# One transformer block pair on one core: the last 64 tokens' expert rows gathered by index and summed by VectorE

## What is computed

```
q = (h @ w_q)                              # per token and head, two halves of 128
s = q . subkeys                            # 16 score rows of 128 per token
v, i = top_k(s, 16)                        # per score row
cand = v[0][:, None] + v[1][None, :]       # 256 pairs per head
tv, tj = top_k(cand, 16)
eidx = i[0] * 128 + i[1] at tj             # 128 experts per token
w = softmax(tv)
a = gelu(h . w_down[eidx])
out = sum over the picks of (w * a) * w_up[eidx]
x = x + gate * out ; result = rms_norm(x) * g
```

## Time and profile before

| | us |
|---|---|
| runs of the kernel, median of 3 | 1251.74 |
| lowest and highest run | 1247.74, 1253.19 |
| span of the profiled execution | 1246.6 |
| TensorE busy | 1197.3 |
| VectorE busy | 900.8 |
| ScalarE busy | 619.8 |
| GpSimd busy | 548.6 |
| down stage with selection, 474 to 886 us | 412.0 |
| up stage, 886 to 1232 us | 346.0 |

### The profile page before, as it was taken

The page is one execution under the profiler, slowest core; times in us unless marked ns, Lnnn a source line. Parts: engine busy times, 40 slices in busy tenths (PEclk is TensorE's granted clock), DMA queues, the critical chain, the costliest instruction groups (busy, mean ns, idle before and its releaser), DMA issues.

```text
span 1246.6 us, 19173 instructions
## 1 busy us (share of the span) xinstructions
PE 1197.3 (96%) x7224; PEld 1047.8 (84%) x7224; DVE 900.8 (72%) x1844; ACT 619.8 (50%) x1079; POOL 548.6 (44%) x323
## 2 busy tenths in 40 slices
PE   4999999999998999999999999999999999999996
PEld 2778877776776899999999999999888888888885
DVE  5678656787886626999668999999566656656666
ACT  1545444454635435444556665555545545545453
POOL 0887759584533015888867777766200000000000
PEclk9999999999999999999999999999999999999998
DMA  9978764354421542555545555444566667666654
GB/s 377 416 315 341 283 275 172 136 210 148 186 89 68 216 155 88 186 185 186 182 142 166 155 158 165 153 153 153 169 227 228 191 224 227 192 190 192 195 193 152
DMA packets 54523, 244.28 MB, mean 196 GB/s; under 512 B 6944, under 2 KB 7328, under 8 KB 42016
## 3 DMA queue, kind: packets, MB, share of 16 engines
q1 hardware_dynamic: 54000, 242.34, 56.3%
q10 hardware_dynamic: 432, 0.72, 0.2%
HBM read 240.94 MB, written 2.10 MB: 195 GB/s over the span
## 4 chain that ended last, share of the span: by engine, by line
PE 88%; DVE 6%; issue 2%; POOL 1%; ACT 1%; DMA 1%; SPq 0%; POOLq 0%; DVEq 0%; ACTq 0%
PE bank L1546 10%; PE bank L1547 10%; PE bank L1550 10%; PE banks L1586 5%; PE bank L1586 5%; PE bank L1589 5%; PE banks L1592 5%; PE bank L1592 5%; PE banks L1589 5%; PE banks L1560 3%; PE banks L1140 2%; PE banks L1146 2%; PE bank L1140 2%; PE bank L1146 2%; PE banks L1152 2%; PE bank L1152 2%
## 5 line engine op out<-in xcount | busy, mean ns | idle before, releaser
L769 POOL TENSOR_TENSOR split_r<-ring,split_r 128x1024 fp32r<-128x1024 f32 x128 | 307.6, 2404 | 156.6 <-ACT split_r L823 156.6
L823 ACT ACTIVATE split_r<-ring 128x1024 fp32r<-128x1024 f32 x256 | 269.1, 1052 | 182.4 <-PE bank L1550 182.4
L1546 PE MATMUL bank<-h_high_r,split_r 128*128 128x256 f32 x1024 | 252.3, 284 | 0.7 <-issue 0.7
L1547 PE MATMUL bank<-h_low_r,split_r 128*128 128x256 f32 x1024 | 252.0, 284 | 0.0
L2170 DVE TENSOR_TENSOR split_r<-ring,split_r 128x1024 fp32r<-128x1024 f32 x128 | 156.8, 1225 | 65.6 <-ACT split_r L823 65.6
L1546 PEld LDWEIGHTS bank<-h_high_r,split_r 128*128 128x128 f32 x1024 | 197.3, 193 | 0.9 <-ACT G L993 0.9
L1547 PEld LDWEIGHTS bank<-h_low_r,split_r 128*128 128x128 f32 x1024 | 197.6, 193 | 0.0
L773 POOL TENSOR_TENSOR small<-small 128x1 f32<-128x1 f32 x2 | 1.5, 760 | 358.7 <-DVE small L2196 358.7
L744 POOL TENSOR_TENSOR wq_low_r<-G,G_r 128x512 fp32r<-128x512 f32 (+1 forms) x104 | 135.0, 1333 | 47.8 <-ACT G_r L818 47.8
L1550 PE MATMUL bank<-h_high_r,split_r 128*128 128x256 f32 x1024 | 143.7, 283 | 0.0
L1059 ACT ACTIVATE gs_r<-G 128x256 fp32r<-128x256 f32 x128 | 53.5, 418 | 172.6 <-PE bank L1592 172.6
(11 more groups left out here) (444 smaller groups left out, 2234.1 us busy)
## 6 DMA issues: line engine op xcount, KB each, us to landing
ring<-in_down SPq DMA_DIRECT2D x128, 512.0 KB, 3.5
ring<-in_up SPq DMA_DIRECT2D x128, 512.0 KB, 3.5
G<-in_ada SPq DMA_DIRECT2D x32, 1024.0 KB, 10.3
G<-in_in SPq DMA_DIRECT2D x32, 1024.0 KB, 7.0
G<-in_out SPq DMA_DIRECT2D x8, 1024.0 KB, 7.1
G<-in_wq SPq DMA_DIRECT2D x8, 1024.0 KB, 7.6
tab<-in_ada SPq DMA_DIRECT2D x4, 1024.0 KB, 6.3
G<-in_poolup SPq DMA_DIRECT2D x2, 1024.0 KB, 6.0
```

Source lines behind the costliest of these rows:

```text
L769: pool.tensor_tensor(wsplit[:, j % SPLIT, 1, :], raw[:, j % RAW, :], wsplit[:, j % SPLIT, 0, :].bitcast(F32), ALU.subtract).then_inc(low_r ...
L823: nc.scalar.activation(wsplit[:, n % SPLIT, 0, :], raw[:, n % RAW, :], ACT.Copy).then_inc(high_ready, 1)
L1546: mm(o, w[0][:, c, :], h_high[:, c, :], start=(c == 0), stop=False)
L1547: mm(o, w[0][:, c, :], h_low[:, c, :], start=False, stop=False)
```

## The change

The last 64 of 256 tokens (`FEW`) leave the dense up stage; 192 (`TD`) stay.

- The one-hot weights are built for 192 tokens only: 48 batches instead of 64, from column 44 (`J0`) instead of 53. So the selection is wanted nine columns earlier.
- `top16` takes two searches at a time and interleaves their steps, so that each step waits for the last but one instruction instead of the last.
- In the down stage ScalarE writes the activations of the last 64 tokens to a small buffer of 8 columns (`stage`), which SyncE stores to HBM (`z_few`, 256 KB each, 16 stores).
- VectorE names the picks of these tokens: row numbers of `w_up` and places in `z_few` (`name_few`; 128 partitions = 2 groups of 64 picks x 64 tokens).
- GpSimd issues 64 transfers by index of 128 rows of 4 KB (`fetch_row`, 512 KB each, 6 buffers; six of them in the down stage) and 64 of 128 single numbers (`take`).
- VectorE multiplies and adds each fetched row to `row_sum` (`add_row`, 128x1024), in 64 of the columns 8 to 118, folds the two groups at columns 122 and 124.
- The up stage has 10 matmuls per column: the first 128 tokens keep three products for each column half; for the other tokens one 128-wide operand holds the high parts of 64 tokens and their low parts side by side, and two products per half give all. The low part of the activations is written by two instructions, 64 and 128 wide.
- Of the 128 low parts of the weights GpSimd writes each third, VectorE the others.
- At the end the second token half comes first, with a copy by ScalarE and an addition by VectorE for each of its column halves.

```diff
@@ -47,13 +47,28 @@
 RAW = 4
 SPLIT = 2
 BATCH = 4
-NB = T // BATCH
-J0 = 53
+FEW = 64
+TD = T - FEW
+REP = P // FEW
+NB = TD // BATCH
+J0 = 44
+STAGE = 8
+ROW_BUFFERS = 6
+TAKE = 8
+SUM_COLUMN = [8 + 7 * k // 4 for k in range(FEW)]
+EARLY_ROW = [100 + 2 * k for k in range(ROW_BUFFERS)]
+ROW_COLUMN = [SUM_COLUMN[k] + 1 for k in range(FEW - ROW_BUFFERS)]
+TAKE_COLUMN = [1 + k // 2 for k in range(TAKE)]
+TAKE_COLUMN += [SUM_COLUMN[TAKE * (k // TAKE - 1)] + 1 + k % TAKE for k in range(TAKE, FEW)]
+FOLD_COLUMN = 122
+LATE_ORDER = [(1, 0), (1, 1), (0, 0), (0, 1)]
 LAST_BATCH = P - 4
 GATE_LOAD = [10 + 16 * k for k in range(4)]
 GATE_SUM = [20 + 16 * k for k in range(4)]
 GATE_ROW = [48, 80]
 GATE_ADD = [54, 86]
+POOL_UP = [n for n in range(P) if n % 3 == 2]
+DVE_UP = [n for n in range(P) if n % 3 != 2]
...
                 if n - RAW < P:
                     sp.wait_ge(low_ready, n - RAW + 1)
                 else:
-                    sp.wait_ge(up_low, n - RAW - P + 1)
+                    wait_up_low(sp, n - RAW - P)
                 src = d["down"][n] if n < P else d["up"][n - P]
                 sp.dma_start(raw[:, n % RAW, :], src).then_inc(raw_in[n % RAW], 16)
+                if RAW + STAGE - 1 <= n < P + RAW and (n - RAW + 1) % STAGE == 0:
+                    m = (n - RAW + 1) // STAGE - 1
+                    sp.wait_ge(gelu_done, STAGE * (m + 1))
+                    sp.dma_start(z_few[:, m * STAGE:(m + 1) * STAGE, :], stage[:, m % 2]).then_inc(z_stored[m % 2], 16)
...
+            def fetch_row(k):
+
+                b = k % ROW_BUFFERS
+                if k == 0:
+                    pool.wait_ge(few_named, 3 * REP)
+                    pool.wait_ge(selT_full, 1)
+                if k >= ROW_BUFFERS:
+                    pool.wait_ge(row_used, k - ROW_BUFFERS + 1)
+                pool.indirect_dma_start(row_buffer[b], None, up_rows,
+                                        bass.IndirectOffsetOnAxis(ap=row_id.bitcast(U32)[:, k:k + 1], axis=0)).then_inc(row_fetched[b], 16)
+
+            def take(k):
+
+                m = k // TAKE
+                if k == 0:
+                    for half in range(2):
+                        pool.wait_ge(z_stored[half], 16 * (P // STAGE // 2))
+                if k % TAKE == 0 and m >= 2:
+                    pool.wait_ge(few_weighed, m - 1)
+                pool.indirect_dma_start(row_z[:, k:k + 1], None, z_cells,
+                                        bass.IndirectOffsetOnAxis(ap=z_id.bitcast(U32)[:, k:k + 1], axis=0)).then_inc(z_taken[m % 2], 16)
...
-            for t in range(NT):
-                pool.wait_ge(var_ready, 6 + t)
+                if j in EARLY_ROW:
+                    fetch_row(EARLY_ROW.index(j))
+            for n in range(P):
+                if n in POOL_UP:
+                    pool.wait_ge(high_ready, P + n + 1)
+                    pool.tensor_tensor(wsplit[:, n % SPLIT, 1, :], raw[:, n % RAW, :], wsplit[:, n % SPLIT, 0, :].bitcast(F32),
+                                       ALU.subtract).then_inc(up_low_pool, 1)
+                for k in range(FEW):
+                    if TAKE_COLUMN[k] == n:
+                        take(k)
+                if n in ROW_COLUMN:
+                    fetch_row(ROW_BUFFERS + ROW_COLUMN.index(n))
+            for k, t in enumerate((1, 0)):
+                pool.wait_ge(var_ready, 6 + k)
...
+                    nc.scalar.activation(zbuf[:, 0:done], src[:, 0:done], ACT.Gelu_apprx_tanh)
+                if done < TD:
+                    nc.scalar.activation(Gv[:, j, done:TD], src[:, done:TD], ACT.Gelu_apprx_tanh)
+                if j % STAGE == 0 and m >= 2:
+                    act.wait_ge(z_stored[m % 2], 16 * (m // 2))
+                ins = nc.scalar.activation(stage[:, m % 2, j % STAGE, :], src[:, TD:T], ACT.Gelu_apprx_tanh)
...
+            def up_parts(n):
+
+                g, w = gs[n % 2], wsplit[:, n % SPLIT]
+                first, both, first_low = g[:, 0:P], g[:, P:2 * P], g[:, 2 * P:3 * P]
+                halves = [(half, slice(half * 512, (half + 1) * 512)) for half in range(2)]
+                return first, both, first_low, w, halves
+
             def up(n):
 
-                outs = [(ps[4 + 2 * t + half][:, :], slice(t * P, (t + 1) * P), slice(half * 512, (half + 1) * 512))
-                        for t in range(NT) for half in range(2)]
-                g, w = gs[n % 2], wsplit[:, n % SPLIT]
+                first, both, first_low, w, halves = up_parts(n)
                 pe_.wait_ge(gs_high, n + 1)
                 pe_.wait_ge(high_ready, P + n + 1)
-                for k, (o, tok, cols) in enumerate(outs):
-                    if n == 0 and k == 2:
-                        pe_.wait_ge(z_done, late_columns(P - 1))
-                    mm(o, g[0][:, tok], w[:, 0, cols], start=(n == 0), stop=False, skip_group_check=True)
-                pe_.wait_ge(gs_low, n + 1)
-                for o, tok, cols in outs:
-                    mm(o, g[1][:, tok], w[:, 0, cols], start=False, stop=False, skip_group_check=True)
-                pe_.wait_ge(up_low, n + 1)
-                for o, tok, cols in outs:
-                    ins = mm(o, g[0][:, tok], w[:, 1, cols], start=False, stop=False, skip_group_check=True)
+                for half, cols in halves:
+                    mm(ps[4 + half][:, :], first, w[:, 0, cols], start=(n == 0), stop=False, skip_group_check=True)
+                if n == 0:
+                    pe_.wait_ge(z_done, late_columns(P - 1))
+                pe_.wait_ge(gs_low, 2 * n + 1)
+                for half, cols in halves:
+                    mm(ps[6 + half][:, :], both, w[:, 0, cols], start=(n == 0), stop=False, skip_group_check=True)
+                pe_.wait_ge(gs_low, 2 * n + 2)
+                for half, cols in halves:
+                    mm(ps[4 + half][:, :], first_low, w[:, 0, cols], start=False, stop=False, skip_group_check=True)
+                wait_up_low(pe_, n)
+                for half, cols in halves:
+                    mm(ps[4 + half][:, :], first, w[:, 1, cols], start=False, stop=False, skip_group_check=True)
+                for half, cols in halves:
+                    ins = mm(ps[6 + half][:, :], both, w[:, 1, cols], start=False, stop=False, skip_group_check=True)
                 ins.then_inc(col_done, 1)
...
+            def top16(*several):
+
+                done = [0] * len(several)
+                for step in range(5):
+                    lo = slice(0, 8) if step < 3 else slice(8, 16)
+                    for k, (values, best, where) in enumerate(several):
+                        if step:
+                            dve.wait_ge(dve_chain, done[k])
+                        if step in (0, 3):
+                            ins = nc.vector.max(best[:, lo], values)
+                        elif step == 2:
+                            ins = nc.vector.match_replace(values, best[:, lo], values, LOWEST)
+                        else:
+                            ins = nc.vector.max_index(where[:, lo], best[:, lo], values)
+                        done[k] = mark(ins)
+                dve.wait_ge(dve_chain, done[-1])
...
             dve.sem_inc(wexp_in, 1)
+
+            def name_few(dst, src):
+
+                for r in range(REP):
+                    ins = nc.vector.tensor_copy(dst[r * FEW:(r + 1) * FEW, :], src[TD - P:P, r * FEW:(r + 1) * FEW])
+                    ins.then_inc(few_named, 1)
+
+            link(stt(out=flat, in0=sel3[:, 1, 1, :], scalar=float(P), in1=sel3[:, 0, 1, :], op0=ALU.mult, op1=ALU.add))
+            name_few(row_id.bitcast(U32), flat)
+            dve.wait_ge(few_named, REP)
+            link(ts(flat, sel3[:, 0, 1, :], float(P * FEW), table("lane"), ALU.mult, ALU.add))
+            link(stt(out=flat, in0=sel3[:, 1, 1, :], scalar=float(FEW), in1=flat, op0=ALU.mult, op1=ALU.add))
+            name_few(z_id.bitcast(U32), flat)
             dve.wait_ge(wexp, 1)
...
+            def add_row(k):
+
+                b, m = k % ROW_BUFFERS, k // TAKE
+                if k % TAKE == 0:
+                    part = slice(k, k + TAKE)
+                    dve.wait_ge(z_taken[m % 2], 16 * TAKE * (m // 2 + 1))
+                    dve.wait_ge(few_named, 3 * REP)
+                    tt(row_w[:, part], row_w[:, part], row_z[:, part], ALU.mult).then_inc(few_weighed, 1)
+                    dve.wait_ge(few_weighed, m + 1)
+                dve.wait_ge(row_fetched[b], 16 * (k // ROW_BUFFERS + 1))
+                if k == 0:
+                    ins = ts(row_sum, row_buffer[b], row_w[:, 0:1], None, ALU.mult)
+                else:
+                    dve.wait_ge(row_used, k)
+                    ins = stt(out=row_sum, in0=row_buffer[b], scalar=row_w[:, k:k + 1], in1=row_sum, op0=ALU.mult, op1=ALU.add)
+                ins.then_inc(row_used, 1)
+
             for n in range(P):
+                g = gs[n % 2]
                 dve.wait_ge(gs_high, n + 1)
```

(29 more changed lines are left out.)

134 lines of the change are left out of this document (77 added, 57 removed).

## The result

The changed kernel takes 1267.6 us (median of four runs, 1265.7 to 1271.3) against 1249.8 us before (four runs): a ratio of 1.0152, with a 95% interval of 1.0130 to 1.0175. The forecast was 1241.

What follows compares the result with a forecast made beforehand. TensorE, busy 96% of the span, was taken as the bound. -8.8 + 0 - 6.4 + 3 + 1.7 = -10.5 us on the profiled 1246.6 gave 1236.1, or 1241 us against the median; range 1205 to 1272.

Steps and rivals of the forecast that it cites:

- Part 1, the batches: Down stage: 16 fewer one-hot weights batches at 0.55 us each, -8.8 us.
- Part 2, the pairs: Selection: interleaved searches gain 0.115 us per step, 27.6 us, so VectorE is ready at 585.4 us; 0 us net.
- Part 3, exclusion: Up stage: VectorE instructions with two SBUF operands and GpSimd tensor instructions exclude each other; 2.61 us a column, -6.4 us.
- the start: Start of the up stage: takes wait for the last store, so column 5's split is late, +3 us.
- the first rival: Up stage: exclusion costs much less than summed, 7.2 us per three columns, 1207 us in all; chance 0.23.
- Part 3, the issues: Up stage: GpSimd's transfers by index at 1.1 us per issue, covered up to 1.5 us each, 0 us.
- The second rival: Up stage: GpSimd's queue becomes the bound from 1.5 us per issue, splits behind issues late, 1265 us; chance 0.23.
- The clock: TensorE's many short waits lower its clock, 5 to 20 us more; chance 0.12 together with the pairs failing.
- Bytes: Up stage: weights and fetched rows need 307 GB/s, where one early stretch moved 410 GB/s; covered.
- Part 4, the end: Kernel's end: one matmul less, but a ScalarE copy and more VectorE instructions in the chain, +1.7 us.

Runs made afterwards that it cites:

- experiment 5: The changed kernel with each search step waiting for the instruction directly in front of it, so the searches are not in pairs: 1283.9 us, ratio 1.027.
- Experiment 11: The changed kernel without transfers by index in the up stage, row sums at full width reading the six rows fetched in the down stage: 1235.9 us, ratio 0.990.
- experiment 8: The changed kernel without any transfers by index and without row sums, each third split still on GpSimd: 1207.7 us, ratio 0.966.
- experiment 10: The changed kernel with all its transfers by index, but each row sum made over 1 of 1024 columns: 1241.3 us, ratio 0.996.
- experiment 4: The changed kernel without the 64 transfers that fetch single activations and the waits for them: 1244.1 us, ratio 0.996.
- Experiments 13 and 16: The changed kernel with every sixth split (21) on GpSimd, 1232.5 us; and with only the 25 GpSimd splits having more than two issues nearby, 1252.6 us.
- experiment 1: The changed kernel with all splits of the up stage on VectorE, none on GpSimd: 1206.2 us, ratio 0.966.
- experiment 3: The changed kernel with all splits of the up stage on VectorE and the row sums kept in PSUM: 1204.4 us, ratio 0.964.

## Why the prediction was wrong

**Part 1, the batches (-8.8): right.** 85 columns from 42 to the last down column take 24.5 us more than 85 x 2.88, for 48 batches: 0.51 us each, predicted 0.55. With 35.2 us for the 64 of before that saves 10.7 us.

**Part 2, the pairs (0): right, with a little more.** VectorE is done at 582.4, predicted 585.4, and experiment 5 puts the gain per step at (607.4 - 582.4) / 240 = 0.104 us, predicted 0.115. It puts the pairs at 16.3 us, predicted 17.5 for the stop without them. The stop at the selection is 3.0 us, not 4.5 (TensorE's wait of 2.10 us for VectorE, at 625.00 before, is gone), and the stage was 1.5 us ahead by then: 10.7 + 1.5 + 1.5 makes the 13.8 us (to rounding) in place of 8.8. By the rule of the Trainium skill's page "VectorE: DVE Perf Modes", section "The DRAIN you can't avoid", that dropping the semaphores gains nothing, experiment 5 would have taken after's time: the runs decide against it where, as here, two chains of searches are interleaved.

**Part 3, exclusion: right in kind and near in size.** Experiment 11 is what this part's sum describes without its issues: 1235.9 us, where the forecast less the 3 us of the start gives 1238. A part of that nearness is luck, since parts 1 and 2 gave 5 us more than forecast. Between columns 8 and 118 three columns take 8.18 us in it, where 7.83 and the 16 gate sums make 8.12; experiment 8, without row sums, gave 7.45, and the first rival had 7.2. The mechanism is there too: in these 300.0 us of experiment 11 VectorE or GpSimd is busy for 290.0.

**Part 3, the issues: this is the step that failed.** It reads: "it is covered up to 1.5 us per issue". Experiment 11 against after puts the issues at 31.7 us where the sum had 0 and 3 us at the start. Two things were wrong in it. The size: 1.1 us was taken, 1.49 measured. The larger one is the test itself. By it even 1.49 is covered: 16 x 1.49 + 13.5 = 37.3 us of the 37.8 in 14 columns. But it averages a queue that TensorE meets at single places. What counts is where GpSimd stands when a split's high copy is ready. The forecast had itself worked out that the room there was negative: the split ends at 3.96 us, the products want it at 3.63. So what is still ahead of the split at that moment can't be covered, while issues that end before it cost nothing: in after 23 of 42 splits start on time, and where those of columns 11, 14, 17 and 32 start 1.54, 1.04, 2.79 and 1.57 us late, TensorE waits 1.69, 1.20, 2.93 and 1.73 us. Lateness at the split's start follows the issues: 0.84 us on average in after, 0.69 with issues and hardly any sums (experiment 10), 0.18 without the activations' issues (experiment 4), 0.08 with none (experiments 8 and 11). 42 x (0.84 - 0.08) = 32 us, the price by experiment 11. For experiment 10 over 8 the same product gives 26 of 33.6 us; 10 has 20 us at the lower clock and 8 none, so lateness with what follows from it fits, but that it is all isn't shown. Experiments 13 and 16 say the same from the other side: half the splits still cost 43% of the 61 us, and a split among many issues costs 1.86 us against 1.19.

**The second rival had the right sign, and half of the mechanism; its time, 1265 us, is luck.** It asked for over 1.5 us per issue as a load, and by its own sum the measured 1.49 us costs nothing (its 13 to 25 us for 1.6 to 1.7 us come out as 10 to 23). Its sentence on a split behind two issues that is late for TensorE is what happened, and issues do wait for VectorE. After, issues and VectorE side by side:

```profile
883.07 0.94 POOL L829 DMA_INDIRECT tab<-z_few,tab  x1 [0.30 <-issue]
...
963.76 0.97 POOL L829 DMA_INDIRECT tab<-z_few,tab  x1 [0.16 <-issue]
963.82 1.21 DVE L2308 TENSOR_TENSOR split_r<-ring,split_r 128x1024 fp32r<-128x1024 f32 x1
964.96 1.27 DVE L2298 SCALAR_TENSOR_TENSOR G<-G,tab 128x1024 f32<-128x1024 f32 x1
965.04 2.01 POOL L829 DMA_INDIRECT tab<-z_few,tab  x1 [0.30 <-issue]
```

Alone, or begun 0.06 us ahead of VectorE, an issue takes 0.94 to 0.97 us. Begun 0.08 us behind a two-operand instruction it takes 2.01: it ends 0.82 us after that one. From 880 us on all 67 issues of after that take over 1.0 us end 0.78 to 0.87 us after a VectorE instruction. The page "SBUF — State Buffer" of the Trainium skill, section "Who interferes with whom", infers that descriptor generation needs the write side and so is not touched by these instructions. The rows decide against that for these issues, whose indices lie in SBUF.

**The start (+3): near.** Six issues from 880.55 to 887.75 stand ahead of column 5's split, and TensorE waits 2.59 us for it.

**The clock (5 to 20 us): came, as a companion.** The forecast gave it little since "the new waits are under 1 us". With late splits they are not. From 880 to 1225 us TensorE waits over 2 us eight times in after; at six of these the clock falls to 1.2 GHz, and a seventh time at the wait of 1.92 us shown above. In experiment 8 no wait is over 1.25 us, and its granted clock is 1.00 from 890 to 1150 us. The 14 us above are a part of the 60 us between the two, not a cost beside them.

**Bytes (covered): right in after,** where ScalarE waits 1.7 us for transfers. In the faster versions they are no longer covered (24.8 us of ScalarE's time in experiment 1, of which 8.2 us reach TensorE), which is one reason why these stay 20 us above TensorE alone.

**Part 4, the end (+1.7):** +2.3.

What stays open: why the activations' 64 issues cost 23.5 us and the 58 row fetches only the remaining 8.2, and the some 6 us by which lateness and move fall short of after's 61.4.

**The best version** is that of experiment 3: the same change, with the splits left on VectorE and the row sums in PSUM. It takes 1204.4 us, 3.6% less than before.

## What to carry to other kernels

Whether a queue covers its work isn't a matter of the average. Where the bounding engine meets a helper's result at one place in each column, take the room at that place (when its input is ready, how long it takes, when it is wanted); if that is near zero or negative, whatever is still ahead in the helper's queue when its input is ready goes to the end in full. And when work is moved to a second engine to relieve one that looks full (6.6 of 6.8 us per three columns by experiment 1's expectation), first run the version without the move: here that engine did it all, 61 us faster, and was busy for 91% of the time (264.1 of the 290 us from 890 to 1180).
